# First loads reordered, first weights in two halves, first token tile projected ahead of the others' transposes

## The reference

```python
def rmsnorm(x, g):
    xf = x.astype(jnp.float32)
    xf = xf * lax.rsqrt(jnp.mean(xf * xf, axis=-1, keepdims=True) + RMS_EPS)
    return (xf * g.astype(jnp.float32)).astype(x.dtype)

def layer_forward(x, pos, h0_re, h0_im, mem_k, mem_v, past_ckv, past_kpe, p):
    h = rmsnorm(x, p["g_attn"])
    proj = h @ p["w_in"]
    ...
    u, q_lat, kv_lat = proj[..., :o1], proj[..., o1:o2], proj[..., o2:o3]
    k_pe, q_mem, g_logit = proj[..., o3:o4], proj[..., o4:o5], proj[..., o5:]
    br_a, h_re, h_im = s5_branch(u, h0_re, h0_im, p)
    ...
    merged = gates[..., 0, :] * br_a + gates[..., 1, :] * br_b + gates[..., 2, :] * br_c
    x = x + merged @ p["w_out"]
    x = x + hierarchical_moe(rmsnorm(x, p["g_ffn"]), p)
    return x, c_kv, k_pe, h_re.astype(x.dtype), h_im.astype(x.dtype)
```

## Time and profile before

| what | us |
| --- | --- |
| runs | 635.49, 637.30, 637.98 |
| median of the runs | 637.3 |
| span of the profiled execution, first to last instruction | 636.0 |
| PE busy in it | 607.9 |
| first transfer issued | 0.70 |
| first transpose of data on PE | 7.25 |
| first product with w_in on PE | 11.15 |
| first product with u1 on PE | 21.83 |

### The profile page before, as it was taken

One profiled execution on the slowest core, in us unless ns is written; L12 is line 12 of the kernel. 1 busy time (PEld: TensorE's weight loads), 2 busy tenths in 40 slices (PEclk: granted clock), 3 DMA queues, 4 the chain that ended last, 5 costly groups with the idle time before them and its releaser, 6 DMA issues.

```text
span 636.0 us, 10034 instructions
## 1 busy us (share of the span) xinstructions
PE 607.9 (96%) x3742; PEld 376.9 (59%) x3742; DVE 321.1 (50%) x858; ACT 184.0 (29%) x579; POOL 149.2 (23%) x341
## 2 busy tenths in 40 slices
PE   8999999999999999999999999998999999997894
PEld 7888867677456667667677767854343343333341
DVE  3343947757883589772043322685425336335133
ACT  5534224532478445422100101211121121120100
POOL 1596627733584525510000000000000000000000
PEclk9999999999899999999999999999999999999999
DMA  9893553212301343322489990089999999999993
GB/s 299 182 290 108 190 174 100 68 66 85 113 2 33 120 146 100 100 67 99 152 252 398 406 392 17 24 375 403 419 419 419 421 421 419 419 419 420 419 407 105
DMA packets 57715, 150.57 MB, mean 237 GB/s; under 512 B 12352, under 2 KB 40448, under 8 KB 45760
## 3 DMA queue, kind: packets, MB, share of 16 engines
q1 hardware_dynamic: 57664, 149.89, 63.1%
HBM read 147.12 MB, written 2.76 MB: 236 GB/s over the span
## 4 chain that ended last, share of the span: by engine, by line
PE 90%; DVE 4%; DMA 2%; issue 2%; ACT 1%; SPq 0%; DVEq 0%
PE PS L832 28%; PE PS L842 21%; PE PS L1216 9%; PE PS L1113 7%; PE PS L1255 5%; PE PS L1245 5%; PE PS L958 2%; PE PS L915 2%; DVE X L2117 2%; PE PS L983 2%; PE PS L825 1%; PE PS L1166 1%; PE PS L1025 1%; PE PS L966 1%; DMA W<-in_w_in 1%
## 5 line engine op out<-in xcount | busy, mean ns | idle before, releaser
L832 PE MATMUL PS<-hT,W 128*128 128x320 f32 x416 | 117.2, 436 | 0.0
L832 PEld LDWEIGHTS PS<-hT,W 128*128 128x128 f32 x416 | 77.5, 190 | 33.5 <-issue 3.8
L1216 PE MATMUL PS<-E,xT 128*32 128x256 f32 (+1 forms) x1088 | 61.4, 376 | 6.5 <-issue 6.2
L1216 PEld LDWEIGHTS PS<-E,xT 128*32 128x32 f32 x1088 | 36.1, 108 | 35.7 <-issue 16.7
L2191 POOL TENSOR_SCALAR means<-sums 128x4 f32<-128x4 f32 (+3 forms) x35 | 7.8, 222 | 187.6 <-ACT junk L1358 186.6
L1113 PE MATMUL PS<-h,S 128*128 128x512 f32 (+1 forms) x96 | 48.2, 625 | 0.7 <-DVE S L1974 0.7
L1255 PE MATMUL PS<-yb,WG 128*128 128x512 f32 (+1 forms) x96 | 40.9, 623 | 4.1 <-DVE X L2117 3.1
L842 PE MATMUL PS<-W,hT 128*128 128x256 f32 (+5 forms) x256 | 41.7, 353 | 0.0
L2117 DVE TENSOR_TENSOR X<-X,PS 128x512 f32<-128x512 f32 (+1 forms) x48 | 32.9, 686 | 8.4 <-PE PS L1255 6.8
L842 PEld LDWEIGHTS PS<-W,hT 128*128 128x128 f32 (+1 forms) x256 | 31.5, 163 | 8.4 <-issue 1.3
L842 PE MATMUL PS<-W,mergedT 128*128 128x384 f32 (+3 forms) x192 | 35.7, 381 | 0.0
(11 more groups left out here) (313 smaller groups left out, 976.9 us busy)
## 6 DMA issues: line engine op xcount, KB each, us to landing
E<-in_w_e SPq DMA_DIRECT2D x93, 1024.0 KB, 22.0
W<-in_w_in SPq DMA_DIRECT2D x7, 1536.0 KB, 7.3
W<-in_w_in SPq DMA_DIRECT2D x7, 1024.0 KB, 8.0
W<-in_w_mem_kv SPq DMA_DIRECT2D x4, 1024.0 KB, 6.2
W<-in_w_glu SPq DMA_DIRECT2D x4, 768.0 KB, 7.6
W<-in_w_out SPq DMA_DIRECT2D x2, 1536.0 KB, 15.1
X<-in_x_prompt SPq DMA_DIRECT2D x4, 512.0 KB, 4.4
W<-in_w_o_mem SPq DMA_DIRECT2D x1, 1536.0 KB, 6.5
```

Of the source, the lines that this page charges most:

```text
L832: ins = mm(out[:, 0:TOK], w[:, k, cols:cols + 128], rhs[:, k, :], start=(k == 0), stop=(k == kt - 1))
L1216: ins = mm(PS[r:r + B, 2 + par, 128 * which.start:128 * which.stop], xT[:, k, place_ + B * n:place_ + B * n + B], E13[slot][:, which, k, j ...
```

## The change

SP's first issues get another order: x0, identity, first half of u0 (k = 0 to 3), gains, x1, second half of u0, x2, u1. The wait for x0 on SP is gone. u_part waits for one half of the weights at k = 0 and for both at k = 4. On PE both u_parts of x0 come right behind the transposes of x0 (and their dummy products), and the transposes of x1 and x2 come behind them. On ACT the sums of squares of x1 and x2 move behind the emptying of x0. On DVE x_rows of the first half of x1 moves behind x_copy of x0. The unit ("u", 1) gets bank 5.

```diff
--- before.py
+++ after.py
@@ -548,6 +548,8 @@
 
 
         def bank(key):
+            if key == ("u", 1):
+                return PS[:, BU, :]
             return PS[:, UNIT_NO[key] % RING, :]
 
         def emptied_at(n):
@@ -570,6 +572,8 @@
             dst = chunk_view(name)
             cols = CHUNKS[CHUNK_NO[name]][2]
             first = {"u0": C_U, "u1": C_U + 256, "ql": C_QL, "kv": C_KV, "qm0": C_QM, "qm1": C_QM + 256}
+            if name == "u0":
+                return [(dst[:, k0:k0 + 4], w_in[:, k0:k0 + 4, C_U:C_U + cols]) for k0 in (0, 4)]
             if name in first:
                 return [(dst, w_in[:, :, first[name]:first[name] + cols])]
             if name[:2] in ("mk", "mv"):
@@ -623,14 +627,21 @@
                 for dst, src in chunk_source(CHUNKS[n][0]):
                     sp.dma_start(dst, src).then_inc(chunk_loaded[SLOT_OF[n]], 16)
 
-            for t, (f, n) in enumerate(TILES):
-                src = xp[f:f + n, :] if t < 2 else xs
-                sp.dma_start(X0[0:n, t, :], src).then_inc(s[f"x{t}_loaded"], 16)
-                if t == 1:
-                    sp.dma_start(cst[:, 0:128], a["consts"][:, 0:128]).then_inc(s["ident_loaded"], 16)
-            sp.wait_ge(s["x0_loaded"], 16)
+            def load_x(t):
+                f, n = TILES[t]
+                sp.dma_start(X0[0:n, t, :], xp[f:f + n, :] if t < 2 else xs).then_inc(s[f"x{t}_loaded"], 16)
+
+            def load_first(half):
+                dst, src = chunk_source("u0")[half]
+                sp.dma_start(dst, src).then_inc(chunk_loaded[SLOT_OF[0]], 16)
+
+            load_x(0)
+            sp.dma_start(cst[:, 0:128], a["consts"][:, 0:128]).then_inc(s["ident_loaded"], 16)
+            load_first(0)
             sp.dma_start(gx[:], a["g_attn"][0].rearrange("(p k) -> p k", k=KD)).then_inc(s["gx_loaded"], 16)
-            load_chunk(0)
+            load_x(1)
+            load_first(1)
+            load_x(2)
             load_chunk(1)
             for n, name in enumerate(("ssm_a_re", "ssm_a_im")):
                 sp.dma_start(s5raw[:, n, :], a[name][0].rearrange("(q g) p -> q (g p)", g=2)).then_inc(s["s5_loaded"], 16)
@@ -820,8 +831,10 @@
 
             def u_part(m, f, n):
 
-                w, out = use("u0"), bank(("u", m))
+                w, out = chunk_view("u0"), bank(("u", m))
                 for k in range(KD):
+                    if k % 4 == 0:
+                        pe.wait_ge(chunk_loaded[SLOT_OF[0]], 16 * (k // 4 + 1))
                     ins = mm(out[:, f:f + n], w[:, k, 128 * m:128 * m + 128], hT[:, k, f:f + n], start=(k == 0), stop=(k == KD - 1))
                 return ins
 
@@ -852,14 +865,13 @@
                 end(ins)
 
             x_turned(0, 0, 2)
-            x_turned(1, 0, 0)
             begin(("u", 0))
             emptied(("xT", 0, 0))
             emptied(("xT", 0, 1))
             u_part(0, *TILES[0])
+            u_part(1, *TILES[0])
+            x_turned(1, 0, 0)
             x_turned(2, 0, 0)
-            begin(("u", 1))
-            u_part(1, *TILES[0])
             emptied(("xT", 2, 0))
             emptied(("xT", 2, 1))
             end(u_part(0, 128, TOK - 128))
@@ -1360,15 +1372,20 @@
                     for q in parts:
                         junk_at[q] = m
 
-            for t, (f, n) in enumerate(TILES):
+            def x_sumsq(t):
                 act.wait_ge(s[f"x{t}_loaded"], 16)
-                sumsq(("x", t), [X0[0:n, t, :]])
+                sumsq(("x", t), [X0[0:TILES[t][1], t, :]])
+
+            x_sumsq(0)
             act.wait_ge(s["gx_loaded"], 16)
             for t, (f, n) in enumerate(TILES):
                 src = full(("xT", t, 1))
                 for k in range(4):
                     ins = fn(hT[:, 4 + k, f:f + n], src[:, k * n:k * n + n], ACT.Copy, scale=gx[:, 4 + k:5 + k])
                     st.mark(ins, s["emptied_act"] if k == 3 else None)
+                if t == 0:
+                    x_sumsq(1)
+                    x_sumsq(2)
             act.wait_ge(s["s5_loaded"], 16 * 5)
             fn(s5raw[:, 4, :].rearrange("q (g p) -> q g p", g=2), dtraw[:, :, None].broadcast_to([GP, 2, ST]),
                ACT.Exp).then_inc(s["s5_raw_ready"], 1)
@@ -1670,9 +1687,9 @@
                 V_.memset(wB[:, 0].rearrange("p t s -> p (t s)")[:, n::2], x).then_inc(s["warm_ready"], 1)
             x_rows(0, 0)
             x_rows(0, 1)
-            x_rows(1, 0)
             dve.wait_ge(s["gx_loaded"], 16)
             x_copy(0)
+            x_rows(1, 0)
             x_rows(1, 1)
             x_rows(2, 0)
             x_copy(1)
```

## The result

Eight runs of each kernel give a median of 639.03 us for the changed kernel (637.39 to 641.13) and 635.9 us for the kernel before. The ratio is 1.0043, with a 95% interval of 1.0028 to 1.0057: by the ratio the change costs 2.7 us (635.9 x 0.0043), 1.8 to 3.6; the two medians stand 3.1 apart. The forecast was 0.8 us slower, and 638.1 us with a range that holds the measured time. But 638.1 stands on a base of 637.3, the median of three runs; from 635.9 the same 0.8 gives 636.7, which is 2.3 us short.

The account below looks back on a forecast made before the run. PE bounds, with 90% of the last-ending chain. Start 1.55 us sooner, less 1.15 transposes, less about 1.2 waiting, gives 0.8 later: span 636.0 to 636.8, plus 1.3, 638.1 us; range 636.2 to 640.0.

Parts of the forecast that it names:

- The order on PE costs more than the early start gives: PE's head: first projection 1.55 us sooner, against 1.15 of x1's transposes and about 1.2 waiting for x2's emptying.
- the lost cover: PE ahead of the 192-token part: without u_part of m = 1 over ACT's emptying of x2, about 1 us idle.
- the rate of 363 GB/s: Loads behind the first half of u0: 1.44 us per 512 KB, x1 at 7.2, second half 8.6, x2 9.4.
- the weights should not hold it: First u_part on PE: k = 4 comes at 10.6, after the second half of u0 lands at 8.6.
- The low rate of 4.10 to 7.20: Transfers in the kernel before: 245 GB/s because u0 was issued late, a hole that the change closes.
- the rival of late weights: The halves of u0 land no earlier than u0 before; 1.4 us slower in place of 0.8, 638.7 us; chance 0.10.
- a sign of being wrong: In the profile after: a wait for W inside the first u_part, meaning late weights.
- x2's norm: DVE's input for x2's transposes: first half ready at 13.4, second at 15.25 behind x_copy of x1.
- To the end: Behind the 192-token part's start at 16.9 all work is as before, so 0.8 us is passed on.
- The clock: Rival: half clock behind the transposes at 16.9 costs 1.65 us, giving 639.8 us; chance 0.15.
- The sum: Head of PE: 1.55 sooner, less 1.15 and about 1.2, puts the 192-token part at 16.9, 0.8 us later.
- the prediction's mark: Start of the 192-token part on PE, 16.09 us in the kernel before; behind it order and work stay the same.

Follow-up runs that it names:

- the cover put back: Changed orders with the old loads, but u_part of m = 1 for x0 put back behind x2's transposes; 636.79 us, ratio 1.0010 to the kernel before.
- the orders alone: Changed orders on PE, ACT and DVE and the new bank, with the loads and wait of the kernel before; 639.18 us, ratio 1.0047.
- the third profile of the kernel before: The kernel before, unaltered, run for one more profile; 635.51 us, span 633.7, mean clock 0.999.
- the second profile: The changed kernel run again without an edit: 639.37 us, ratio 1.0047; its profiled execution took 640.87 us at mean clock 0.993.
- the kernel with SP held: The changed kernel with SP held behind u1's issue until x2 has landed; 637.85 us.

## Why the prediction was right, and where not

- *The order on PE costs more than the early start gives:* right. The first projection came 1.42 us sooner (1.55 forecast), the idle time behind x2's transposes was 1.07 (about 1 forecast). The runs with the cover put back and with the orders alone show the two prices: 1.23 for x1's transposes on the path (1.15 forecast) and 0.97 for the lost cover.
- *The loads:* wrong. The step that failed is the rate of 363 GB/s taken for all that is queued, and with it "the weights should not hold it". "The second half at 8.6" measured 10.8, "x2 at 9.4" 12.0. Of the 2.2 us of the second half, 1.2 are x2's own slow transfer, as moving x2 behind u1 brings the landing to 9.6. The other 1.0 is there without x2: the first half, put at 5.7, landed at 6.7 to 7.3 in all seven profiles with the new loads, and why stays open. The low rate of 4.10 to 7.20, read as a hole because u0 was issued late, was only in part one: in the kernel before without the wait, whose queue is full, the rate from 6 to 7 us is still only 193 and 212 GB/s in its two profiles. So the rival of late weights, which had 0.10, came true: the second half landed at 10.8 and 11.8 in the changed kernel's two profiles, about when u0 did (11.02) or later. It held the first u_part for 0.26 and 0.89 us, which the prediction itself had named as a sign of being wrong. In the first profile the sum hardly shows it, by luck: the forecast gave each u_part 1.96 us, and two in a row take 3.64.
- *x2's norm:* late by x2's landing, which cost PE another 0.20 us. With 9.73 for 9.6 at the start the 192-token part came at 17.33 in place of 16.9.
- *To the end:* right, the head's shift is passed on whole.
- *The clock:* a rival with a chance of 0.15, which came true in a part of the executions, at the place and about the price given (4.22 - 2.77 = 1.45 us in the 192-token part alone; 1.65 forecast). The sentence of the Trainium skill, page "TensorE: Matmul & The Clock Gate", section "Part 4: PE-mode transpose", that the full clock doesn't engage for transposes, is in line with one profile of the changed kernel at 19.6 us and not with the other; no run separates the transposes from the idle time between them. Against the rival I had set that the stretch of 3.4 us was shorter than the 5.2 at 166; that argument failed. How often it happens is open, as each execution tells only its mean clock; the two groups of times put it, or the fall at 166, into most of fourteen of nineteen.
- *The sum:* 0.8 was too small for 2.7. Between the first profiles the head takes 1.38 (u1 at 23.21 against 21.83), but the prediction's mark was itself on the late side: in the third profile of the kernel before u1 starts at 21.46, with no idle time ahead of the first projection that an earlier start could win. Among executions with a mean clock of 0.998 or more the change costs 2.1 us; by these few, most of the 2.7 is in the head. The 0.6 left over are the clock and, in some executions, weights that land up to 1 us later still (the wait of 0.89 in the second profile). How these two share it is not measured.
- *The time:* 638.1 came within 0.9 us of 639.03 by luck. The change cost about 2 us more than forecast, and the base it was added to stood 1.4 us too high (637.3 from three runs, 635.9 from eight). Moved by as much, the range would have ended at 638.6, below the measured time.

## What to carry to other kernels

Before work is moved ahead, ask what it was covering: u_part of m = 1 hid the emptying of x2, and the transposes of x1 cost nothing while PE waited for weights. A low transfer rate behind a late issue may be a slow transfer and not a hole; see whether the DMA engines are busy in it, move that transfer and see whether the low rate follows. And a stretch of transposes and short idle times that one execution passes at full clock may halve the clock in the next, so a single profile of a reordered head isn't enough.

## What the runs showed of the hardware

The 256 KB of x2 (64 rows of 4 KB, into 64 partitions) come with a rate of 140 to 215 GB/s with all DMA engines busy, and what moves beside them slows down with them: the second half of the weights, queued ahead of x2, lands at 10.8 to 11.8 with x2 right behind it and at 9.6 with x2 behind u1. In that last kernel the rate is 344 to 376 from 5 to 11 us, ahead of x2. (One microsecond of the changed kernel's first profile, 5 to 6, has 189 GB/s with busy engines too, and no run says why.) The granted clock fell to half after 3.8 us of transposes and idle time (14.62 to 18.39), about 1.2 us into the products that followed, in one execution; after 3.7 us (13.63 to 17.33) in another, and 3.8 us (14.37 to 18.16) in the kernel with SP held, it didn't fall.
